# One VectorE step of a chunked scan reordered: the normalisation first

## The reference, cut to what matters

```
def step(state, inp):                       # one chunk, all groups
    decay = exp(where(causal, seg, -inf))
    cb = einsum('bign,bjgn->bgij', cc, bc)
    y_diag = einsum('bgij,bgrij,bjgrp->bigrp', cb, decay, xc)
    y_off = einsum('bign,bgrpn->bigrp', cc, state) * exp(cum)
    new_state = state * exp(total) + einsum(bc, w_tail, xc)
...
y = (ssd_chunked_scan(...) + dsk * xs) * silu(z)
yg = yg * rsqrt(mean(yg * yg) + eps)        # per token and group
out = yg * norm_w
```

## Time and profile before

| | |
|---|---|
| runs, median (lowest to highest) | 2492.35 us (2489.95 to 2492.69) |
| profiled execution, its time | 2492.35 us |
| profiled execution, span from first to last instruction | 2491.1 us |
| mean granted TensorE clock | 0.987 |
| PE, DVE, ACT, POOL busy | 2268.2, 935.4, 701.4, 585.6 us |

### The profile page before, as it was taken

The page is one execution under the profiler, slowest core; times in us unless marked ns, Lnnn a source line. Parts: engine busy times, 40 slices in busy tenths (PEclk is TensorE's granted clock), DMA queues, the critical chain, the costliest instruction groups (busy, mean ns, idle before and its releaser), DMA issues.

```text
span 2491.1 us, 32460 instructions
## 1 busy us (share of the span) xinstructions
PE 2268.2 (91%) x13108; PEld 1683.9 (68%) x13108; DVE 935.4 (38%) x1797; ACT 701.4 (28%) x1361; POOL 585.6 (24%) x685
## 2 busy tenths in 40 slices
PE   7999999999999989988788788888779999999999
PEld 5776888888888565554444444444448777888887
DVE  5667677776423240110000110000035575542441
ACT  4546556565221010000000000000022465431330
POOL 4443466675100111111111111111013250000000
PEclk9999999999999999999999999999989998999999
DMA  7332343343436489999999999999981201222221
GB/s 186 97 81 62 94 132 105 106 148 127 167 121 259 159 346 427 426 427 427 426 426 426 426 427 426 427 426 427 428 322 62 94 27 51 85 102 102 102 95 41
DMA packets 149593, 575.47 MB, mean 231 GB/s; under 512 B 14972, under 2 KB 75928, under 8 KB 124736
## 3 DMA queue, kind: packets, MB, share of 16 engines
q1 hardware_dynamic: 126576, 530.58, 53.8%
q0 software_dynamic: 16288, 28.98, 3.4%
q10 hardware_dynamic: 6576, 13.77, 1.8%
HBM read 562.69 MB, written 31.52 MB: 239 GB/s over the span
## 4 chain that ended last, share of the span: by engine, by line
PE 60%; DMA 28%; DVE 7%; issue 2%; ACT 2%; POOL 0%; ACTq 0%; DVEq 0%; POOLq 0%
PE ps L684 14%; PE ps L686 13%; PE ps L685 13%; DMA ringx<-in_w_expert_gate 7%; DMA ringx<-in_w_expert_up 6%; PE ps L1041 6%; DMA ring<-in_w_expert_up 4%; DMA ring<-in_w_expert_gate 4%; PE ps L1067 3%; PE ps L943 2%; PE ps L677 2%; DMA ringx<-in_w_expert_down 2%; DMA ringy<-in_w_expert_gate 2%; DMA ringy<-in_w_expert_up 1%; PE ps L1206 1%
## 5 line engine op out<-in xcount | busy, mean ns | idle before, releaser
L2263 DVE TENSOR_TENSOR hid<-ps,sg 128x256 f32<-128x256 f32 x64 | 27.2, 425 | 824.0 <-issue 808.7
L684 PE MATMUL ps<-hTh,hb 128*128 128x512 f32 x576 | 236.3, 410 | 3.0 <-DVE ringr L1834 3.0
L1041 PE MATMUL ps<-ringx,gxT 128*64 128x256 f32 x1664 | 199.3, 391 | 40.2 <-DMA ringx<-in_w_expert_up 24.4
L686 PE MATMUL ps<-hTh,ringr 128*128 128x512 f32 x576 | 226.8, 394 | 0.0
L685 PE MATMUL ps<-hTl,hb 128*128 128x512 f32 x576 | 226.2, 393 | 0.0
L1622 ACT COPY ys<-ps 128x512 f32<-128x512 f32 x64 | 37.4, 585 | 623.8 <-PE ps L1067 623.8
L1041 PEld LDWEIGHTS ps<-ringx,gxT 128*64 128x64 f32 x1664 | 134.2, 135 | 113.2 <-issue 65.9
L1834 DVE TENSOR_TENSOR ringr<-ring,hb 128x1024 fp32r<-128x1024 f32 x112 | 150.4, 1345 | 91.8 <-ACT hb L1349 91.0
L2672 POOL DMA_INDIRECT gx<-h2d,rows x64 | 65.5, 1024 | 507.0 <-PE ps L677 441.2
L1041 PE MATMUL ps<-ring,gxT 128*64 128x256 f32 x1216 | 147.3, 393 | 30.3 <-DMA ring<-in_w_expert_up 20.5
L1041 PE MATMUL ps<-ringy,gxT 128*64 128x256 f32 x1216 | 145.3, 390 | 26.7 <-DMA ringy<-in_w_expert_up 17.0
(11 more groups left out here) (459 smaller groups left out, 4674.2 us busy)
## 6 DMA issues: line engine op xcount, KB each, us to landing
ringx<-in_w_expert_gate SPq DMA_DIRECT2D x26, 2048.0 KB, 45.6
ringx<-in_w_expert_up SPq DMA_DIRECT2D x26, 2048.0 KB, 46.0
ringx<-in_w_expert_down SPq DMA_DIRECT2D x25, 2048.0 KB, 46.2
ring<-in_w_expert_down SPq DMA_DIRECT2D x19, 2048.0 KB, 45.8
ring<-in_w_expert_gate SPq DMA_DIRECT2D x19, 2048.0 KB, 46.2
ring<-in_w_expert_up SPq DMA_DIRECT2D x19, 2048.0 KB, 45.9
ringy<-in_w_expert_down SPq DMA_DIRECT2D x19, 2048.0 KB, 46.0
ringy<-in_w_expert_gate SPq DMA_DIRECT2D x19, 2048.0 KB, 45.3
```

The source lines that it names most:

```text
L684: pe.matmul(o, lh, rh, start=start and n == 0, stop=False)
L686: m = pe.matmul(o, ll, rh, start=False, stop=stop and n == len(ks_) - 1)
L1041: m = pe.matmul(b[c * 64:c * 64 + 64, 0:256].rearrange("p (n j) -> p n j", j=2), gxTs[e % 2][:, k % 4, k // 4 * 64:k // 4 * 64 + 64], w4[: ...
```

## The change

In `dve_scan` the piece for yn (c = n - 5) is moved from between the state and the y products to the top of the step. The two pieces for c = n - 3 become one. No instruction is added, removed or altered, and the programs of the other engines stay as they are.

```diff
@@ dve_scan
+        c = n - 5
+        if 0 <= c < 4:
+            q = 4 * gr + c
+            v.wait_ge(*at("r2", q + 1))
+            if gr >= 2 and c == 0:
+                v.wait_ge(*at("yT", 2 * gr - 2))
+            v.tensor_scalar(yns[gr % 2][:, c, :], yys[q % 2][:, 0, :], st2s[q % 4][:, 1:2], None, MUL).then_inc(s["yn"], 1)
         c = n - 2
         if 0 <= c < 4:
             q = 4 * gr + c
@@
         c = n - 3
         if 0 <= c < 4:
-            k = 3 * gr + c
+            q, k = 4 * gr + c, 3 * gr + c
+            y, xd, b = yys[q % 2], xds[q % 2], banks[4 + q % 2]
             if c < 3:
                 new = stas[k % 3]
@@
                     v.tensor_tensor(new[:, :], new[:, :], banks[6][:, 0:256], ADD).then_inc(s["st"], 1)
-        c = n - 5
-        if 0 <= c < 4:
-            q = 4 * gr + c
-            v.wait_ge(*at("r2", q + 1))
-            if gr >= 2 and c == 0:
-                v.wait_ge(*at("yT", 2 * gr - 2))
-            v.tensor_scalar(yns[gr % 2][:, c, :], yys[q % 2][:, 0, :], st2s[q % 4][:, 1:2], None, MUL).then_inc(s["yn"], 1)
-        c = n - 3
-        if 0 <= c < 4:
-            q = 4 * gr + c
-            y, xd, b = yys[q % 2], xds[q % 2], banks[4 + q % 2]
             v.wait_ge(*at("yd", q + 1))
```

## The result

The changed kernel takes 2512.97 us (median of 4 runs, 2512.43 to 2517.07), beside 2491.48 us (2489.95 to 2492.69) for the kernel before. The two medians are 21.5 us apart; forecast were 18.9, and 2511 us for the time. Nine further executions of the changed kernel are on record, and the median of all thirteen is 2511.63 us, 20.2 above 2491.48. The recorded ratio, 1.0082 with a 95% interval of 1.0069 to 1.0095, stands for 20.4 us (17 to 24). So the loss is 20 to 21 us. The profiled execution took 2511.63 us for a span of 2510.3; against the profiled execution of before that is 19.3 us more.

The account below looks back on a forecast made before the run. In the scan stage TensorE was taken as the bound, waiting without slack for VectorE's state sum. 2492.35 + 11.9 (delay, seven groups) + 7.0 (clock falls) = 2511.25, stated as 2511 us, range 2501 to 2524.

Parts of the forecast that it names:

- The root comes 0.50 us earlier: POOL's root r2, which yn waits for, gains 0.33 + 0.17 us without E*mask and L2000 beside it.
- The later start of the state sum: On VectorE, L2001 starts at 394.94 against 393.37, 1.57 us later, behind the waiting yn and E*mask.
- the rival by which all groups do the same: Clock falls in nearly every group, or E*mask also meets POOL's next root: 2516 to 2530 us, chance 0.22.
- step (d): Whether E*mask on VectorE meets POOL's next root: delay 1.57 if not, 2.1 if so; 1.7 us taken per group.
- Nothing absorbs it: After the scan stage TensorE has no gap from 640 to 820 us, and the expert-weight loads start as much later.
- The clock: TensorE's 2.3 us gaps in the scan stage halve its clock after four of seven, 1.75 us each: 7.0 us.
- The last group: The eighth group adds nothing: VectorE idles 2.37 us for L853 anyway, and yn and E*mask fit in between.
- The delay alone: Rival: TensorE's waits lengthen but its clock stays up, 2503 to 2505 us; chance 0.19 for 2500 to 2506.
- The change does not matter: Rival: TensorE's wait at L841 takes it up or later stages give it back; 2492 us, chance 0.07.
- Faster: Rival: out of POOL's way E*mask and L2000 shorten and TensorE's seven 0.60 us gaps close; 2488 us, chance 0.02.

Follow-up runs that it names:

- e3: Changed kernel with 18 identity transposes on TensorE ahead of its wait for the state of chunk 2, in groups 0 to 6: 2503.62 us, ratio 1.0044.
- e4: Kernel before, with yn of chunk 0 put first in groups 0 to 2 only: 2501.72 us, ratio 1.0038.
- e1: Changed kernel with POOL's root of chunk 0 ahead of the three xd products of chunk 3: 2495.57 us, ratio 1.0010.
- e5: Kernel before, with the state of chunk n-3 ahead of E*mask of chunk n-2 in each step: 2485.02 us, ratio 0.9976.
- e6: Kernel before, with the edits of e5 and e1 together: 2485.75 us, ratio 0.9984.
- e7: Changed kernel as in e3, but with 8 transposes in place of 18: 2503.06 us, ratio 1.0057.

## Why the prediction was right

- **Only one instruction in each group moves.** In VectorE's program the only exchange is that of yn of chunk 0 with E*mask and the state at step 5. The programs of the other engines are the same.
- **The root comes 0.50 us earlier, and E*mask and the state take less.** From POOL's first xd product to yn it is 3.99 us (394.12 to 398.11) where it was 4.48, so 0.49 earlier. L2608 takes 0.61 and L2550 0.23, as taken from the earlier trace rows; E*mask 0.69, L2008 0.42. The later start of the state sum, worked out as 1.57, is 1.57.
- **One reading was too exact.** The cycle of the kernel before was said to repeat every 44.2 us to within 0.03. From one long wait to the next it is 44.36, 44.21, 44.23, 44.21, 44.31 and 44.55 us. Nothing in the sum rests on the 0.03, but it stood behind the rival by which all groups do the same, and the clock did not do the same in all.
- **The unknown of step (d), the next root beside E*mask,** was the one term that was too large: 0.13 us was added for it, and nothing came. POOL's L2551 has its start at 398.36, 0.01 before E*mask, but it is POOL's that is stretched (1.12 in place of 0.56) and E*mask's 0.69 is not. The Trainium skill ("SBUF — State Buffer", section "SBUF: two separate sides") has the one that starts first keep the port pair. By the start in the row that would be POOL, and the delay 2.1; the trace does not agree with the rule read off these starts, though it does with one of the two being held up by the other. Here it is POOL that was held up, as it was beside the L1834 of 402.42 in the kernel before. Forecast for seven groups 11.9 us; the waits in the profile say 10.7, e3 says 11.0.
- **Nothing absorbs it.** e3 shows the seven delays and e4 about three sevenths of the whole loss in the total time, and the expert weights start 18.3 us late.
- **The clock.** Forecast were four falls at 1.75 us, 7.0 in all; the profiled execution has five at 1.6, which is 8, and with e3 the medians put it at 9 to 10. The granted clock of the scan stage is 0.97, a little below the forecast 0.98 to 0.99. Both terms were off by little and in opposite directions, delay and clock together 18.9 against 18.7; that the two errors cancel so well is luck, and so in part is the count, taken as four of seven from seven pauses elsewhere. e3 shows that this term is real and not a part of the delay.
- **The last group** loses nothing, as forecast: its yn waits 2.05 us, and L2008 behind it still waits for L853.
- **The rivals.** "The delay alone" is e3's time, 2503.62, inside its 2503 to 2505. "The change does not matter" fails at L841, where 0.60 became 2.18. "Faster" would have needed the root 1.57 us earlier. e1 gives that and much more, and still gains nothing on the kernel before: yn itself then meets POOL.

## What to carry to other kernels

On an in-order engine, an instruction takes its wait along when it is moved up, and everything behind it inherits it. So before moving one up, look at when its input is ready, then at who waits for the instructions that it overtakes. An engine that is busy for 73% of a stage (VectorE, 247 of the 340 us from 300 to 640) can still be the one that the bound engine waits for at one point of the cycle; there the order should be by who is waited for, as in e5, and an idle time that nobody waits for (e6) is worth nothing. A pause of TensorE has to be priced with the clock behind it: here 1.6 us of added pause cost about 3 us.

## What the runs showed of the hardware that was not expected

Seven pauses of TensorE of the same length (2.17 to 2.20 us), in the same place of the same cycle, had different sequels: behind five the granted clock was at about half for some 3.4 us, behind two it stayed at 1.00. e4's profiled execution has a fall behind a pause of 1.50 us and none behind one of 2.17. The length of a pause alone does not decide it, and what does was not found. A fall also does not always cost its 1.6 us: where a wait for another engine follows, as in group 0 of e4, the wait takes it up. e4's runs spread over 7.3 us and e7's over 6.8, those of e5 over 4.1. That this spread comes from how many pauses are followed by a fall fits the profiled execution of e4, but was not shown for its other runs.
